# A two-block, four-layer forward pass on one core: key products and output turns of the delta pairs, branch a's taps and the first constants in another order

## What is computed

```
first block, each of 2 layers:
    h += 0.5 * rms_norm(swiglu(rms_norm(h)))
    a_b, a_c, a_x, b_u, c_q, ..., gate_logits = split(rms_norm(h) @ w_in)
    y_a = (a_b * causal_depthwise_conv(a_c * a_x, 3 taps)) @ a_w_out      # branch a
    y_b, y_c, y_d = long convolution, differential attention, forgetting attention
    h += rms_norm((sum of sigmoid(gate_i) * y_i) @ w_o)
    h += 0.5 * rms_norm(swiglu(rms_norm(h)))
second block, each of 2 layers:
    x = layernorm(ALPHA * x + 0.5 * swiglu_2(x))
    y = hybrid_mixer(x)          # windowed attention and the gated delta rule, 8 heads
    x = layernorm(ALPHA * x + y);  x = layernorm(ALPHA * x + 0.5 * swiglu_2(x))
delta rule, per head and chunk: t_inv = (I + strict(k k^T * decay))^-1, u = t_inv v, o = q S + (q k^T * decay) u
    o = rms_norm(o) * gain * silu(z)
```

## Time and profile before

| | |
|---|---|
| median of 3 runs | 3132.31 us (3131.12 to 3133.8) |
| the profiled execution | 3131.86 us; span from first to last instruction 3130.1 us |
| PE busy | 3001.0 us, 96% |
| PEld busy | 2832.6 us, 90% |
| DVE busy | 1920.8 us, 61% |
| ACT busy | 1347.3 us, 43% |
| POOL busy | 524.8 us, 17% |
| granted clock of PE, mean | 0.990 |

### The profile page before, as it was taken

The page is one execution under the profiler, slowest core; times in us unless marked ns, Lnnn a source line. Parts: engine busy times, 40 slices in busy tenths (PEclk is TensorE's granted clock), DMA queues, the critical chain, the costliest instruction groups (busy, mean ns, idle before and its releaser), DMA issues.

```text
span 3130.1 us, 54768 instructions
## 1 busy us (share of the span) xinstructions
PE 3001.0 (96%) x22114; PEld 2832.6 (90%) x22114; DVE 1920.8 (61%) x3367; ACT 1347.3 (43%) x2281; POOL 524.8 (17%) x821
## 2 busy tenths in 40 slices
PE   8999999999999999999999988999999999889998
PEld 7999999998989999898998888989989898889897
DVE  5557776556556876646655576466565556664655
ACT  4344454434344554434334543434343355443432
POOL 1000000000000000000003554540000056546000
PEclk9999999999999999999999999999999999999999
DMA  6544445554554466554553322245555432123553
GB/s 228 186 175 163 145 145 183 191 184 180 189 177 174 138 182 180 192 182 175 203 209 128 108 82 68 82 175 192 195 177 215 168 114 102 68 77 140 177 193 131
DMA packets 72861, 498.66 MB, mean 159 GB/s; under 512 B 8320, under 2 KB 8496, under 8 KB 19872
## 3 DMA queue, kind: packets, MB, share of 16 engines
q1 hardware_dynamic: 67824, 471.95, 42.8%
q0 software_dynamic: 4512, 22.20, 2.3%
q10 hardware_dynamic: 272, 0.99, 0.1%
HBM read 490.92 MB, written 4.19 MB: 158 GB/s over the span
## 4 chain that ended last, share of the span: by engine, by line
issue 47%; PE 37%; DVE 8%; POOL 3%; DVEq 2%; ACT 2%; DMA 1%; POOLq 1%; ACTq 0%
PE psum L1259 11%; PE psum L1426 6%; PE psum L1368 4%; PE psum L1650 4%; POOL weights_low L1139 2%; PE psum L1308 2%; DMA weight_ring<-stream 1%; PE psum L1653 1%; DVE work L2574 1%; DVE weights_low L2172 1%; PE psum L1656 1%; PE psum L1394 1%; PE psum L1546 1%; DVEq L2569 1%; PE psum L1754 1%
## 5 line engine op out<-in xcount | busy, mean ns | idle before, releaser
L1832 ACT ACTIVATE weights_high<-weight_ring 128x2048 fp32r<-128x2048 f32 (+5 forms) x774 | 907.4, 1189 | 856.7 <-DMA weight_ring<-stream 856.6
L2172 DVE TENSOR_TENSOR weights_low<-weight_ring,weights_high 128x2048 fp32r<-128x2048 f32 (+5 forms) x528 | 896.7, 1704 | 612.2 <-ACT weights_high L1832 609.8
L1259 PE MATMUL psum<-normed_t_high,weights_high 128*128 128x256 f32 x2560 | 725.1, 283 | 0.0
L1259 PE MATMUL psum<-normed_t_high,weights_low 128*128 128x256 f32 x2560 | 723.9, 283 | 0.0
L1259 PE MATMUL psum<-normed_t_low,weights_high 128*128 128x256 f32 x2560 | 723.9, 283 | 0.0
L1259 PEld LDWEIGHTS psum<-normed_t_high,weights_high 128*128 128x128 f32 x2560 | 490.6, 192 | 3.6 <-issue 0.6
L1259 PEld LDWEIGHTS psum<-normed_t_low,weights_high 128*128 128x128 f32 x2560 | 490.6, 192 | 3.0
L1259 PEld LDWEIGHTS psum<-normed_t_high,weights_low 128*128 128x128 f32 x2560 | 490.7, 192 | 0.0
L1139 POOL TENSOR_TENSOR weights_low<-weight_ring,weights_high 128x256 fp32r<-128x256 f32 x544 | 403.6, 774 | 231.3 <-ACT weights_high L1832 231.2
L1426 PE MATMUL psum<-normed_t_high,weights_high 128*128 128x256 f32 x1248 | 387.2, 310 | 9.2 <-DVE weights_low L2172 9.2
L1426 PE MATMUL psum<-normed_t_low,weights_high 128*128 128x256 f32 x1248 | 357.6, 287 | 0.0
(11 more groups left out here) (279 smaller groups left out, 4645.6 us busy)
## 6 DMA issues: line engine op xcount, KB each, us to landing
weight_ring<-stream SPq DMA_DIRECT2D x400, 1024.0 KB, 4.9
weight_ring<-stream SPq DMA_DIRECT2D x64, 768.0 KB, 4.2
feature_rows<-feat POOLq DMA_DIRECT2D x12, 1024.0 KB, 5.9
work<-toeplitz_rows POOLq DMA_DIRECT2D x8, 512.0 KB, 6.6
toeplitz_rows<-work POOLq DMA_DIRECT2D x16, 192.0 KB, 3.9
params<-prms POOLq DMA_DIRECT2D x5, 239.5 KB, 2.9
residual<-x SPq DMA_DIRECT2D x2, 512.0 KB, 5.1
out<-residual SPq DMA_DIRECT2D x4, 256.0 KB, 2.0
```

Of the source, the lines that this page charges most:

```text
L1259: ins = pe.matmul(PS[:, bank, at:at + S], w[a][:, first + k, c * P:(c + 1) * P], src[b][:, k, :], start=(k, m) == (0, 0), stop=(k, m) == ( ...
L1832: return act.activation(dst, src, ACT.Copy, scale=scale)
L2172: dve.tensor_tensor(some(LOW, i, q, n), some(RING, i, q, n), some(HIGH, i, q, n).bitcast(F32), ALU.subtract).then_inc(low_by_vector, n)
```

## The change

Four edits, in `plan_first`, `plan_start`, `plan_second` and POOL's opening.

1. `gate_a(p)` for p = 1 and 3 returns three `later` steps `tap_a`, one per tap, which hold what `conva` did first; `conva` begins with its product. The instructions are the same.
2. In `plan_start` an idle step is added, and the low part of a unit hangs on the step after the one that its high part hangs on. DVE's order becomes norm 0, norm 1, `xt`, low of unit 0, low of unit 1.
3. In the delta pairs `dot` a and b move from places 3 and 5 of a chain to 8 and 11, and the last two steps of the preparation, `dkk` a and b, no longer stand behind `du4` but three places apart behind `dtf` b.
4. POOL sets its constants first and issues its two transfers after that.

```diff
     def gate_a(p):
-        return pl.make("pa", ("pa", p), ...), []
+        host = pl.make("pa", ("pa", p), ...)
+        return host, [(0, None, lambda n=n: pl.step("tap_a", ("tap_a", p, n), p=p // 2, a=n)) for n in range(3 * (p % 2))]
...
     pl.units, pl.by, pl.low_at = 0, [], []
+    pl.step("idle")
     for n, st in enumerate(pl.steps[T:]):
-        st.high = st.low = [(n, 0, QUARTERS)]
+        st.high = [(n, 0, QUARTERS)] if n < EARLY else []
+        st.low = [(n - 1, 0, QUARTERS)] if n else []
...
         if hp:
             for n in range(2):
-                chain.insert(3 + 2 * n, (2, lambda h=2 * hp - 2 + n: dot(h)))
+                chain.insert(8 + 3 * n, (2, lambda h=2 * hp - 2 + n: dot(h)))
...
-            for n, item in enumerate(todo[:9]):
+            for n, item in enumerate(todo):
                 chain.insert(12 + 3 * n, item)
-            chain += todo[9:] + ends
+            chain += ends
...
-            pool.dma_start(PG[:, 1, :], feat1[0, 3, 1:2, :].to_broadcast([P, D])).then_inc(feature_rows_loaded, 16)
-            pool.dma_start(PRM[:, :], prms[0]).then_inc(params_loaded, 16)
             pool.memset(NC[:, :], 0.0).then_inc(zeros_set, 1)
             pool.drain()
             pool.memset(HALFNEG[:, :], -0.5)
             for eps, at in EPS_AT.items():
                 pool.drain()
                 pool.memset(EPSES[:, at, :], eps)
             pool.drain()
+            pool.dma_start(PG[:, 1, :], feat1[0, 3, 1:2, :].to_broadcast([P, D])).then_inc(feature_rows_loaded, 16)
+            pool.dma_start(PRM[:, :], prms[0]).then_inc(params_loaded, 16)
...
+            def tap_a(st):
+                aw, n = prm("aw", 1, 3), st.a
+                dve.drain()
+                for c in (2 * st.p, 2 * st.p + 1):
+                    w = aw[:, 2 - n, c:c + 1]
+                    if n == 0:
+                        dve.tensor_scalar(ACCA[:, c, :], ZA[:, c, :], w, None, ALU.mult)
+                    else:
+                        dve.scalar_tensor_tensor(out=ACCA[:, c, n:S], in0=ZA[:, c, 0:S - n], scalar=w,
+                                                 in1=ACCA[:, c, n:S], op0=ALU.mult, op1=ALU.add)
             def conva(st):
                 job, c2 = st.jobs[0], 2 * st.p
-                aw = prm("aw", 1, 3)
-                for n in range(3):
-                    dve.drain()
-                    ... (the same two instructions per tap)
                 dve.drain()
                 dve.wait_ge(bank_full[job.bank], full_at(job))
```

More of the change, by code:

```diff
@@ L366, in gate_a @@
     def gate_a(p):
-        return pl.make("pa", ("pa", p), banks=["lo"], signals=[("branch_gate_ready", 1)], p=p, unit=("aa", p)), []
+        host = pl.make("pa", ("pa", p), banks=["lo"], signals=[("branch_gate_ready", 1)], p=p, unit=("aa", p))
+        return host, [(0, None, lambda n=n: pl.step("tap_a", ("tap_a", p, n), p=p // 2, a=n)) for n in range(3 * (p % 2))]
     def value_a(p):
@@ L444, in plan_first @@
     interleave(pl, chain, dense)
+    for p in range(2):
+        assert pl.steps.index(pl.named["tap_a", 2 * p + 1, 2]) < pl.steps.index(pl.named["conva", p])
     pl.steps += [gate(j)[0] for j in range(24, 28)]
@@ L2684, in _ @@
             walk(dve, {"norm": norm, "small_split": small_split, "xt": xt, "gut": gut, "hturn": hturn, "bias_row": bias_row, "gu": gu, "post": post, "lam": lam, "pb": pb, "convb": convb,
-                       "pf": pf, "pa": pa, "conva": conva, "score": score, "diff": diff, "out_norm": out_norm,
+                       "pf": pf, "pa": pa, "tap_a": tap_a, "conva": conva, "score": score, "diff": diff, "out_norm": out_norm,
                        "lnb1": lnb1, "lnb3": lnb3, "out_turn": out_turn, "gy": gy}, 1, low=split_low)
```

## The result

The changed kernel takes 3112.27 us, the kernel before 3133.06 (medians of 4 runs each, taken together): ratio 0.9935, interval 0.9923 to 0.9947, so some 21 us faster, where 24.2 were forecast. The profiled execution took 3112.92, its span is 3111.1. In it PE is busy 2998.3 us, before 3001.0 of 3130.1. So the time in which PE does nothing fell from 129.1 to 112.8, and its busy time, for the same matmuls, by 2.7. PE's lines stand 5 lower in the changed file and the delta pairs' DVE lines 6 lower: L1754 is now L1759, L2661 is L2667, L2649 is L2655.

The account below looks back on a forecast made before the run. The prediction took PE, busy 96% of the span, as the bound, so gains come only from its idle time or clock. 9.2 + 10.6 + 3.6 + 0.8 = 24.2 us off 3132.31 gave 3108.1, range 3100 to 3124.

Parts of the forecast that it names:

- Key products up: Delta pair borders: moving `dkk` ahead removes the waits of `dl0` and `dkk`; gain 9.2 us, between 4.4 and 10.4.
- the residual before `dl0`: Wait left before `dl0` a once `dkk` has moved: 0.2 us a border, 1.2 in all at 6 borders.
- Output turns down: Four borders: moving `dot` behind level 1 removes 17.0 us of waits, 6.4 return; gain 10.6, between 3 and 17.0.
- The 0.5 of `dla` 1 b: New wait of the first level's second `dla` for DVE to end `dl0` b: 0.5 us a border.
- a rival for `du3`: `dkk` before the taps delays ACT's tanh and copies for `du3`, 4.4 us at four borders: slower, 3145.5, chance 0.04.
- The bank 3 wait: New wait of `ddc` a for DVE's first instruction of `dot` b in their shared bank: 0.8 us a border.
- The clock: Low PE clock behind the 2.75 us wait before `dla` goes at two of three borders: 3.6 us, between 0 and 5.4.
- Low parts and POOL's opening: At the start, `weights_low` products 0.4 us earlier and norm 0.2 earlier; together 0.8, between 0 and 1.7.
- Branch a's taps: Layer 0's busy DVE stretch ends when it did, its 2.40 us wait unchanged: gain 0, up to 4.8 either way.
- not all: Rival that everything goes, with all border waits and the low clock removed: 33.6 us gained, 3098.7, chance 0.08.
- moving along: Rival that the `dot` waits shift to the second level's `dlb`; only 9.2 + 0.8 us gained, 3122.3, chance 0.17.
- the key products were a cause: Opposed rival: squares, root and scaling delay `dl0` instead, and `dot` waits move too; 3129.8 us, chance 0.09.

Follow-up runs that it names:

- e3: The kernel before with only the key products (`dkk`) moved to their new place: 3124.77 us, ratio 0.9976 to the kernel before.
- e4: The kernel before with only the output turns (`dot`) moved to their new place: 3113.35 us, ratio 0.9946 to the kernel before.
- e6: e1 with no convolution taps dealt to the four places behind `dl0` and the first level's `dla`: 3115.95 us, ratio 0.9952 to the kernel before.
- e1: The changed kernel with POOL's two opening transfers back in front of its constants: 3110.2 us, ratio 0.9928 to the kernel before.
- e8: e1 with branch a's taps back inside `conva`: 3111.93 us, ratio 0.9937 to the kernel before.
- e9: e1 with the first low parts back in their old order: 3110.45 us, ratio 0.9936 to the kernel before.
- e7: e6 with the taps held back over the first level's `dlb` too, six places: 3113.71 us, ratio 0.9949 to the kernel before.
- e10: e6 with the output turns moved past both `ddc`: 3122.05 us, ratio 0.9971 to the kernel before.
- e11: e1 with the output turns moved past both `ddc`, taps not held: 3117.19 us, ratio 0.9958 to the kernel before.
- e13: e1 with the taps held back at one place only, behind a pair's first `dl0`: 3109.51 us, ratio 0.9931 to the kernel before.
- e5: The changed kernel with the two opening transfers issued on ACT's queue instead of POOL's: 3108.82 us, ratio 0.9928 to the kernel before.

## Why the prediction came out as it did

**Key products up** (9.2): right in size, in part by luck. `dsc` follows the root, the residual before `dl0` is 0.3 at five borders against 0.2 at six, and alone the move took 8.4 (e3). But that is a sum with two terms that were not forecast: the waits of `dl0` and `dkk` fell by 8.8, 4.4 came behind `dl0`, and 3.1 went at `dlb`. The prediction had `dsc` late only because it stands behind `dkk`. That is so, but `dkk`'s 2.18 us on DVE held 1.49 for two masks, made while POOL subtracted (from 1864.01 to 1869.76); in the new place `dkk` b took 1.27 in all. So the move took the meeting with POOL away from `dkk`'s masks (L2639, median 0.76 before; 0.29 after) and gave it to `dl0`. `dkk` in front of the taps made no copy for `du3` late: no row of the changed kernel has that wait.

**Output turns down** (10.6): right in size, in part for other reasons. Behind the moved key products it brought 129.1 - 8.4 - 111.0 - 0.6 = 9.1. The residual was put at 1.6 a border; 0.50 + 0.89 + 0.84 = 2.2 were there. The 0.5 of `dla` 1 b was read from a row in which POOL did not subtract beside `dl0`; the 0.50 came at `dla` 1 a, and of the 0.89 at `dla` 1 b 0.32 is the order on DVE (e4) and 0.57 the longer second instruction. ACT's copy behind the tanh was a rival for `du3` and came at `dlb`, at 0.84 instead of 4.4. The bank 3 wait (0.8) stayed away in the changed kernel, since DVE had done its first instruction of `dot` b 4.4 us after PE began `dot` a, not 5.0; but the mechanism is real: e6 shows it at 2.07, as soon as DVE is that much later.

The sentence on the Trainium skill, SBUF — State Buffer, section Who interferes with whom, was set aside for the rows, and there the rule was the better guide, for an instruction that the prediction did not look at. For the casts it held and cost little: the one beside POOL's subtraction took 0.61, the one without 0.29, and ended 0.15 after the subtraction under way (0.73) had; PE waited for neither. For `dl0`'s second instruction it cost 6.2 us of PE's waiting, more than the 4 us that the prediction named as the price if PE had to wait. That POOL's subtractions make it longer is read from the rows, and from e3, which meets them, and e4, which hardly does; no run took the subtractions themselves away.

**The clock** (3.6): PE's busy time fell by 2.7, but not where it was forecast. Of the four borders that had the 2.75 us wait, three lay in stretches at 0.97. In the changed kernel two do (1923 to 1979 and 2735 to 2791), the second borders of both layers; the first borders (1867 to 1923 and 2679 to 2735) read 1.00. One of these two had read 1.00 before. So at the borders the cost of the lower level in one stretch was won, some 1.7 us (0.03 x 56), not in two. The changed kernel, e1, e8 and e9 have the same waits at the border and PE busy times from 2995.1 to 3000.9. So the term is smaller than its own scatter and nothing was shown of it. Waits of 2.1 at `ddc` or `dot` went with more busy time in e6 and e7 (3005), and not in e10 and e11; what decides that stays open.

**Low parts and POOL's opening** (0.8): this step failed, by 3.2: the first `weights_low` products were to come 0.8 earlier, near 18.5, and came 2.4 later, at 21.68. The low parts' order did what was worked out: PE's wait for `normed_t_low` went from 1.3 to 0, 0.22 came, and with the opening put back (e1) the products start at 18.67, 0.6 earlier than in the kernel before. The opening did not come 0.2 earlier. The prediction let the transfers land as much later as they were issued later, 1.3. In fact the second landed 4.3 later (9.3 to 13.6), and the drain inside the first root waited for it. The first turn is 3.0 late; e1 takes that back. By then x and the first weights were under way from SP's queue, and they landed earlier than before: ACT's last squares started at 6.94, before at 8.99, and its first copy of weights at 9.52, before at 11.32. The Trainium skill, DMA: Bandwidth & Descriptors, section Queues, rings and completion order, says that each DMA engine takes turns between the queues it has work for, packet by packet. The trace is in line with it, as the second transfer went from 7.3 to 10.3 with more of SP's stream issued before it; single packets are not in these rows, and no run held SP's stream back.

**Branch a's taps** (0): right, 2.42 for 2.40, and e8.

By the profiles the span fell by 19.0 and not by 24.2: 8.4 + 9.1 = 17.5 of idle time by the two moves (forecast 19.8), 0.6 by the low parts, less 1.8 for the opening (112.8 - 111.0; its own rows say 3.0, but e1 waits 0.9 longer for low parts of POOL), and 2.7 of busy time (3.6). By the medians it is 20.8; the interval of the ratio is some 7.5 us wide, so the 3.4 us between that and 24.2 are not resolved. The rivals fell: of 25.8 us of waits 10.9 came back, not all, and 6.2 of these not by moving along but from POOL; the key products were a cause; nothing became slower.

## What to carry to other kernels

Before a wait is removed by moving a step, count what the engine behind it does in the whole stretch: e6 and e10 to e13 moved one backlog of DVE from `dla` to `ddc`, to `dot`, to `dtr`, and PE's idle time did not fall (111.2 to 121.2, in e1 111.0). Then look at what a third engine does beside the new place: `dl0`'s second instruction took 0.28 us alone and up to 0.85 beside POOL's subtractions, and the move that took `dkk` out of their way put `dl0` into it. A move pays where it fills a hole of the late engine, as the change did with the 3.89 us of the earlier trace rows, and costs where it opens one. Here a transfer issued 1.3 us later, with a stream started in between, landed 4.3 later, and a drain behind it handed that on to all that followed on the engine.

## What the runs showed of the hardware

A drain on POOL lasted until POOL's own transfers had landed: to 9.49 for a landing at 9.3 (transfers first) and to 13.83 for 13.6 (constants first). It took no such time while transfers of another queue were in flight (e5, 0.74 to 1.96). In e10 and e13 the second transfer landed at 10.4 and 10.1, and the first turn came at 13.9 and 13.5, before at 12.78. The profile shows the drain only as "issue". `dl0`'s DVE instruction with both inputs in SBUF took up to 0.85 us beside POOL's subtractions and 0.28 without; the one with an input in PSUM 0.27 to 0.29 either way. A wait and the low clock are loosely tied: PE's busy time for the same matmuls ranged from 2993.5 to 3005.5 us.
